# Identity products of 512 columns between the last k turns, behind the expert counts and in the pause before the first gathered rows

## The reference, cut to what matters

```
hn   = norm(x) * (1 + sc1) + sh1
u, q, k, v = split(hn @ w_in)               # k is also an output: k_prompt, k_sample
mix  = [pool mixer(u) | stick-breaking attention(q, k, v)] @ w_out
x    = layer_norm(ALPHA * x + (1 + g1) * mix)
hn2  = norm(x) * (1 + sc2) + sh2
# routing: the best of 4 groups, then the best 2 of its 4 experts
g    = argmax(softmax(hn2 @ w_group + b_group))
el   = (hn2 @ w_router + b_router)[group g]
wv, idx = top_k(softmax(el), 2)
# 16 experts, each D=1024 -> 2*256 -> D=1024
y    = sum over the two experts e of a row: ((silu(a_e) * u_e) * gate_e) @ w_down[e]
x    = layer_norm(ALPHA * x + (1 + g2) * y)
```

## Time and profile before

| what | value |
|---|---|
| median of three runs | 807.39 us (805.93 to 811.0) |
| the profiled execution's own time | 804.16 us |
| span of the profiled execution | 802.4 us |
| mean granted TensorE clock | 0.979 of full speed |
| PE busy | 767.7 us, 96% of the span |
| DVE busy | 562.9 us, 70% |
| ACT busy | 374.6 us, 47% |
| POOL busy | 309.9 us, 39% |

### The profile page before, as it was taken

How to read it: one execution, slowest core, us unless ns; L and a number is a source line. 1 busy time by engine, 2 the same in 40 slices (tenths; PEclk the granted TensorE clock), 3 DMA queues, 4 the chain that set the end, 5 groups by cost and what they waited for, 6 DMA issues and landing times. The chain is left out here.

```text
span 802.4 us, 13449 instructions
## 1 busy us (share of the span) xinstructions
PE 767.7 (96%) x4808; PEld 606.4 (76%) x4809; DVE 562.9 (70%) x621; ACT 374.6 (47%) x706; POOL 309.9 (39%) x261
## 2 busy tenths in 40 slices
PE   7999999999989899999999997799999999999995
PEld 4889999999975566767767786488888888888641
DVE  5759957762125995876787867998656999574178
ACT  4571212212246983554464528544444444544254
POOL 2100799990010300100000110367565899564156
PEclk9999999999999999999999996899999999999997
DMA  8947644715049701320202249967779998889695
GB/s 320 388 153 257 210 158 133 228 53 185 1 149 327 236 2 53 106 80 27 80 27 79 80 158 333 338 249 262 259 269 361 415 376 270 294 315 364 238 372 200
DMA packets 78442, 168.59 MB, mean 210 GB/s; under 512 B 6974, under 2 KB 32126, under 8 KB 76219
## 3 DMA queue, kind: packets, MB, share of 16 engines
q1 hardware_dynamic: 69154, 134.36, 47.9%
q0 software_dynamic: 8048, 29.36, 9.9%
q10 hardware_dynamic: 1192, 4.21, 1.5%
HBM read 132.57 MB, written 33.12 MB: 207 GB/s over the span
## 5 line engine op out<-in xcount | busy, mean ns | idle before, releaser
L2501 PE MATMUL psum<-we_hi,x_parts 128*128 x384 | 136.5, 402 | 0.8 <-ACT x_parts L2257 0.8
L2045 DVE TENSOR_TENSOR we_lo<-we_raw,we_hi 128x2048 fp32r<-128x2048 f32 x48 | 118.0, 2461 | 1.5
L490 PE MATMUL psum<-hn_hi,w_hi 128*128 128x364 f32 (+1 forms) x380 | 91.2, 332 | 1.3 <-DVE hn_lo L716 1.3
L490 PE MATMUL psum<-hn_lo,w_hi 128*128 128x364 f32 (+1 forms) x380 | 90.3, 329 | 0.0
L490 PE MATMUL psum<-hn_hi,w_lo 128*128 128x364 f32 (+1 forms) x380 | 90.0, 328 | 0.0
L2044 DVE CAST we_hi<-we_raw 128x2048 fp32r<-128x2048 f32 x44 | 59.6, 1355 | 39.5 <-DMA we_raw<-in_w_up_dram 25.6
L1279 PE MATMUL psum<-wo_hi,mixin 128*128 128x512 f32 (+1 forms) x256 | 82.9, 395 | 1.6 <-DVE logits L1646 1.1
L2501 PEld LDWEIGHTS psum<-we_hi,x_parts 128*128 128x128 f32 x384 | 72.1, 188 | 15.3 <-issue 1.1
L2501 PE MATMUL psum<-we_lo,x_parts 128*128 x192 | 75.4, 393 | 0.0
L793 DVE SCALAR_TENSOR_TENSOR proj<-early,cT,proj 128x2048 f32<-128x2048 f32 x28 | 72.1, 2616 | 1.5 <-DMA early<-in_w_mod_dram 1.3
L490 PEld LDWEIGHTS psum<-hn_hi,w_hi 128*128 128x128 f32 x380 | 66.6, 189 | 4.7 <-issue 2.3
(11 more groups left out here) (376 smaller groups left out, 1569.2 us busy)
## 6 DMA issues: line engine op xcount, KB each, us to landing
we_raw<-in_w_up_dram SPq DMA_DIRECT2D x32, 1024.0 KB, 8.4
early<-in_w_mod_dram SPq DMA_DIRECT2D x16, 1024.0 KB, 5.4
we_raw<-in_w_down_dram SPq DMA_DIRECT2D x16, 1024.0 KB, 7.0
w_raw<-in_w_in_dram SPq DMA_DIRECT2D x16, 512.0 KB, 6.2
we_raw<-ff_d SPq DMA_DIRECT2D x12, 512.0 KB, 7.2
proj<-in_x_prompt_dram SPq DMA_DIRECT2D x4, 1024.0 KB, 8.0
sc_room<-in_w_mod_dram SPq DMA_DIRECT2D x4, 1024.0 KB, 11.0
wo_raw<-in_w_out_dram SPq DMA_DIRECT2D x2, 2048.0 KB, 9.4
```

Of the source, the lines that this page charges most:

```text
L490: mm = pe.matmul(psum[:, 2 * c + slot, 0:n], w[:, slot, k, :], hn[:, k, t0:t0 + n], start=(k == 0 and w is w_hi and hn is hn_hi), stop=(k ...
L2045: dve.tensor_tensor(we_lo[:, a:b], raw, we_hi[:, a:b].bitcast(F32), ALU.subtract).then_inc(ready, 1)
L2501: mm = pe.matmul(psum[:, bank, :], x[:, s, k, :], w[:, bass.ds(at + k * 2 * DE, 2 * DE)], start=(k == 0 and x is x_hi and w is we_hi), sto ...
```

## The change: identity products in three places

A helper `spread_ident(bank, n)` issues n identity products of 512 columns, each the same instruction as in the four of before. It is used in three places:

- After each of the turns t = 4 to 8, one product into bank 6: five products, all ahead of the expert counts in PE's order.
- After the counts and ahead of `by_slot`, three products into bank 4. The wait for the last staged k tile moves up with them, ahead of `by_slot`.
- After `by_slot`, five products into bank 4, where four stood before.

```diff
+            def spread_ident(bank, n):
+
+                for _ in range(n):
+                    pe.matmul(psum[:, bank, :], ident[:, :], ident[:, None, :].broadcast_to([P, 4, P]), start=True, stop=True)
+
             for t in range(K_EARLY, TILES):
                 turn_k(t)
+                if t >= 4:
+                    spread_ident(6, 1)
             pe.wait_ge(r_both, 1)
             pe.wait_ge(act_staged, V_STAGED + K_EARLY)
...
+            pe.wait_ge(act_staged, V_STAGED + TILES)
+            spread_ident(4, 3)
             by_slot(6, ont_ids, 0, 1, True)
-            pe.wait_ge(act_staged, V_STAGED + TILES)
-            for n in range(4):
-                pe.matmul(psum[:, 4, :], ident[:, :], ident[:, None, :].broadcast_to([P, 4, P]), start=True, stop=True)
+            spread_ident(4, 5)
             pe.wait_ge(tables_ready, 1)
```

## The result

| kernel | median of runs | runs | before beside it | ratio, 95% interval |
|---|---|---|---|---|
| the change | 811.85 us (808.88 to 813.33) | 20 | 807.18 us (20 runs) | 1.0055 (1.0040 to 1.0069) |

The kernel became slower by 0.55%, that is 4.4 us of 807.18. The forecast was +3.2 us (810.6), within 1%, with 806.0 to 815.3 as its range. The profiled execution took 810.45 us, with a span of 808.7.

The account below looks back on a forecast made before the run. PE, busy 96% of the span, bounds the kernel; a delayed first expert product reaches the end whole. Terms 4.0 - 0.3 + 0 - 0.2 - 0.3 = +3.2 us on the median 807.39 gave 810.6 us, range 806.0 to 815.3.

Parts of the forecast that it names:

- Part 1: Five products between the k turns, ahead of the counts: clock full at 498.6, counts start 4.0 us later; bounds +2.4, +7.0.
- Part 2: Counts and the three products behind them: counts gain 0.3 us at full clock; products hide in DVE's 4.39 us pause, 0.
- Part 3: by_slot and five products behind it: by_slot gains 0.2 us; products hidden in 6.3 us before the gathered rows land.
- The fetch: Fetch of the gathered rows, 4.88 us before: meets the queues later, perhaps with less ahead; -0.3 us, ends 0 and -1.3.
- two gains, 0.5 together: -0.2 us for by_slot at full clock and -0.3 us for the fetch of the gathered rows.
- The step that had no term: Between by_slot's products and the first expert product: clock 1.00 from 510.71 through the 3.84 us pause, so nothing to save.
- One of my own signs of a wrong forecast: From the first expert product on: the forecast is wrong if the expert stretch itself changes its length.
- Rival (a): At the k turns, ahead of the counts: clock stays half; +7.4 us, 814.8, up to 817; chance 0.17.
- The rule quoted for it: At the k turns: transposes do not count as busy for the clock, so five products might not raise it.
- Rival (b): At the products between the turns: clock already full or rises within the first; +1.4 us, 808.8; chance 0.13.
- Rival (c): At the first expert products: faster, as the change saves half-clock time some runs lose there; -1.8 us, 805.6; chance 0.08.

Follow-up runs that it names:

- the kernel with this part alone: Only the five products between the k turns added to the kernel before, four behind by_slot as there; 811.87 us, ratio 1.0049.
- the doubled dose: Against the change, two products instead of one after each of the turns 4 to 8; 815.25 us, ratio 1.0104 against the kernel before.
- the single one: Against the change, one product between the turns (after t = 4) instead of five; 807.77 us, ratio 1.0028 against the kernel before.
- the transposes: Against the change, twelve identity transposes replace the product after each of the turns 4 to 8; 812.18 us, ratio 1.0079 against the kernel before.
- three and five: Against the change, no products between the turns; three behind the counts and five behind by_slot kept; 808.03 us, ratio 1.0026 against the kernel before.
- three alone: Only the three products behind the counts added to the kernel before; four behind by_slot, none between turns; 808.36 us, ratio 1.0014.

## Why the prediction was right, and where its sizes were off

**Part 1, the delay of the counts, was the main loss.** I put it at +4.0 (the working as written gives 3.9, since 498.6 + 4.1 is 502.7). The trace shows +3.7, and the kernel with this part alone gives 0.49% where the change has 0.55%. The rise came 3.4 us after the first product, as taken, at 500.1 in place of 498.6, since this execution was 1.5 us late before it reached the products. All the rest of the step held: no idle time ahead of the counts, the 4.39 us of DVE unchanged at 4.37, the delay carried to the end. Doubling the dose added 4.0 us, and a single product fitted the 1.49 us of idle.

That the rise came just when I took it was luck. It came 2.4 us after the first product in the kernel with this part alone and in the doubled dose, and 2.6 with the single one; with this part alone the counts started 3.3 us late instead of 3.7. And the clock rose as the turns ended in four of nine traces without any product between them. The term came out near because it depends little on the moment of the rise: in the kernel with this part alone a rise 1.0 us earlier took 0.4 us off it.

**Part 2.** The counts gained 0.3, as taken. The three products hid in DVE's pause, as said. `by_slot` gained 0.0 and not 0.2, since its second half waits for DVE whatever the clock is.

**Part 3.** The five products just fit: 6.25 us with the clock falling as they began and rising 3.5 us later. I had worked out 6.0 for that case. The rows let PE start 0.60 us later, where I had said about 2 us, for products at full clock.

**The fetch** was sized wrong: I took -0.3 and it was +0.5. The first fetch took from 4.88 to 6.10 us in the thirteen traces whose chain of waits holds it, 5.45 in the kernel before run again. That is a spread of executions, of several kernels and of one, and it was no ground for a gain.

**The sum over again.** With what the runs showed, the terms are 3.7 for the delay, -0.3 for the counts and nothing for `by_slot` and the fetch: +3.4. The measured +4.4 has an interval of 3.2 to 5.6 us, so these terms reach it without any other. The forecast of +3.2 lay just as near by a delay taken 0.3 too large and two gains, 0.5 together, that did not come. I had also said that a measurement could barely tell 1% from no change; with 20 runs the interval was about 0.15% to either side.

**The step that had no term** is the one behind the rows. I wrote that nothing could be saved between 510.71 and 514.55 because the clock was at 1.00 there. That was one execution. In another of the same kernel it fell, and the first twelve expert products took 1.4 us longer. One of my own signs of a wrong forecast was that the expert stretch changes its length, and in the two traces compared it did: its first twelve products took 1.6 us more. In all seven kernels that have filling work ahead of `by_slot` (the change, the turns alone, the doubled dose, the transposes, the single one, three and five, three alone) it fell in the trace, with 4.4 to 5.5 us for the twelve. Of the three traces without such work and with the pause open (before, before again, five behind `by_slot`) it held in one. Seven of seven against two of three does not show that the change brings the fall about. Part of the measured loss may lie here, between nothing and about 2 us by the interval above. How large it is stays open: one trace for each kernel is too few to count how often the clock falls in it.

**Rival (a)**, the clock stays at half between transposes, did not come true in any trace with products between the turns: the clock was full at 500.1 in the change, and by 500.4 in the other three, always before the counts. The rule quoted for it, from the Trainium skill, TensorE: Matmul & The Clock Gate, Part 4: PE-mode transpose, does not hold in these runs: in the kernel with further transposes PE made nothing else from 492.5 on and the clock was full at 498.1, and in the kernel before run again it was full at 497.8, right behind the k turns. It did so in four of nine traces with nothing but the k turns there. The trace on which I saw it agree had 4.19 us of transposes at half clock, and so had the second one of the same kernel, only that there the clock rose 0.1 us after their end. I took one execution as a confirmation of the rule.

**Rival (b)**, the clock full from the start, did not occur in the trace of the changed kernel. **Rival (c)** named the right weakness, the first expert products at half clock, and the wrong sign: the change did not protect them. Its products end before the pause behind which the clock is lost.

## What to carry to other kernels

A product that only keeps the clock up delays nothing where the engine would wait for another anyway, and there only up to the length of that wait: ahead of a step on the chain, 1.49 us of idle took one product, and five cost 3.7 us where a little over 2 was at stake. Count the stake first, by the time of the critical products at either level of the clock, and try the filling in the last gaps ahead of them, not in an early one; a gain from that was possible here, about 1.2 us, and not shown. A course of the clock read from one execution is one draw: look at a second trace of the same kernel before you build on it.

## What the hardware showed that I had not expected

- Transposes alone were followed by a rise of the clock, at 498.1, when PE had made nothing else since 492.5. Behind the same k turns, with nothing between them, it rose as they ended in four traces and stayed at half in five.
- Where the clock falls differs between executions of the same kernel: 488.3 in one trace and 491.0 in another, and later either no fall, or one at 501.2 and one at 514.9.
- The clock can be lost at the first expert products whatever the idle time ahead of the rows: it fell about there behind 0.20 to 3.00 us. The twelve products took 5.0 to 5.5 us in the three traces with 2.25, 2.95 and 3.00 us, and 4.4 to 4.6 in the six with 0.20 to 1.90 us. That is a pattern of nine traces with the pause open, and no proof of a cause.
